# Root-mean-square factors of two norms computed on all partitions at once, through a product with ones and a power on GpSimd

## The chip, the cores and the metric

The kernel runs on one core of one Trainium2 chip. The metric is the device time of one execution in microseconds. A core has five engines that run side by side and meet only through semaphores: TensorE (PE) multiplies matrices into PSUM, VectorE (DVE) and ScalarE (ACT) read PSUM and SBUF, GpSimd (POOL) reads SBUF alone, and SyncE (SP) issues most of the transfers. Each takes its instructions in the order in which they are written for it.

## The reference

A two-layer block with sequence length 512 and width 1024: an attention with compressed, selected and windowed keys (NSA) and a latent attention (MLA) side by side, then an MLP. In float32 throughout. The parts that matter here are the norms:

```python
def rms_norm(x, g):
    xf = x.astype(jnp.float32)
    y = xf * lax.rsqrt(jnp.mean(xf * xf, axis=-1, keepdims=True) + EPS)
    return (y * g.astype(jnp.float32)).astype(x.dtype)

# in mla_attention: cq has 256 columns, ckv 128
q = (rms_norm(cq, q_norm) @ w_uq)...
kv = (rms_norm(ckv, kv_norm) @ w_ukv)...

# in reference, per layer
xn = rms_norm(x, attn_norm[l])
...
x = x + merged @ w_out[l]
hn = rms_norm(x, mlp_norm[l])
x = x + jnp.square(jax.nn.relu(hn @ w_up[l])) @ w_down[l]
# at the end
return rms_norm(x, final_norm)
```

## The kernel before

Everything lies transposed: a tile has 128 features on the partitions and the 512 positions along the columns, and x is eight such tiles. Each float32 operand of a product is split into a rounded half (fp32r, "hi") and a rest ("lo"), and `three` makes three products of them (hi·hi, hi·lo, lo·hi). A weight unit is 128x1024 float32, so one output tile of 512 columns is 8 x 3 = 24 products (`tile`, lines 1496 to 1498). SyncE loads units into a double buffer `stage` (the small ones of W1 and W2 into `stage_n`), ScalarE rounds them into `wsplit` (or `narrow`) and VectorE, in places GpSimd, subtracts for the rest (line 992, line 509). The next unit's load waits for that rest.

Per layer the stages are: the prefix (PREFIX in the code: projections KC, VC, KS, V, KW, Q0, CQ0, Q1, CQ1, W1, CQ2, ... up to the first gates, with the units W1,0 to W1,7 of the compression between them), 106 attention steps, the output projections, and the MLP as four quarters of eight "up" tiles and eight "down" tiles. The order on each engine is written out by hand as loops over the same lists.

A norm's factor differs per position, which here is per column, so it must stand on all partitions. Before, it comes about in five steps on four engines:

- the squares are summed over tiles into one 128x512 tile (`row_sum` for x; `csq` for the latents, where GpSimd adds the two tiles of cq, line 569);
- TensorE sums over the partitions: four fp32 products with one column of ones per tile turn the positions onto partitions (`mean_square`, line 1516; `c_mean_squares`, line 1637, eight products);
- ScalarE takes the root of that small block (`root`, line 642; `c_root`, line 738) and VectorE the reciprocal (lines 1026, 1123);
- VectorE writes it onto the diagonals of four 128x128 blocks (`norm_diagonals`, line 1029; `c_diagonals`, line 1127);
- TensorE spreads it over all partitions by an fp32 product of 512 columns with a matrix of ones (`spread`, line 1521; `c_spread`, line 1645, twice), and for x ScalarE copies it into `rs` (line 646). The latents are scaled straight from PSUM in `c_norm` (line 1135).

In the MLP the first quarter's tile 0 is followed by `mean_square`, and `spread` stands before the sixth of tile 1's eight steps. The tiles go into four banks in turn; on VectorE the first evacuation (line 1454: relu times `rs`) waits for `rs`. In its order there stand: the diagonals, the weight rest of tile 2, the wait for `rs`, evacuation 0, the rest of H 0 (line 1460, after ScalarE's square, line 964, and GpSimd's, line 611), evacuation 1, the weight rest of tile 3, and so on.

In the prefix, `c_square` follows each CQ tile, `c_mean_squares` the tile Q2 and `c_spread` the tile MISC. VectorE's order after MISC: evacuate (line 1051), key products, weight rest, query rests (line 996), key sum, the three `c_norm`, then the narrow rest for W1,4; at Q3 the rotation's first half (line 1067), the next weight rest, gates, hidden sum, rotation. GpSimd does the two key rests and the sum of line 569 and then waits to store gates to memory (line 515). The factor of the attention's norm and that of the last norm use the same functions `mean_square`, `root` and, for the first, `spread`.

## Time and profile before

| | |
|---|---|
| median of 3 runs | 1515.47 us (1514.43 to 1516.17) |
| the profiled execution | 1514.82 us, of which span 1513.0 us |
| granted TensorE clock, mean | 0.999 |
| busy: TensorE, VectorE, ScalarE, GpSimd | 1494.5, 891.1, 716.3, 437.5 us |
| instructions in the span | 21119 |

The span runs from the first to the last instruction that the profiler recorded; the rest of the execution's time lies around it. Busy times are sums of the durations of an engine's instructions. TensorE's are modelled and overlap, since products are pipelined: for what a product takes out of the stream the distance from start to start is read, not its duration. GpSimd's durations are rough.

### The profile page before, as it was taken

What the parts mean: (1) busy time and instruction counts of PE and PEld (TensorE: products, weight loads), DVE (VectorE), ACT (ScalarE), POOL (GpSimd) and SP (SyncE); (2) the same over time, 40 slices, a digit from 0 to 9 for tenths busy, and PEclk for the clock granted to TensorE, in tenths of its full rate; (3) what the DMA queues carried; (4) which work ended last, traced back from release to release, by engine and by line L of the source; (5) the groups of instructions that cost most, each with busy time, mean ns of one, the idle gap of its engine ahead of it and who ended that gap; (6) DMA issues with size and microseconds to landing.
All of it is one profiled execution on the core that took longest, in us unless ns stands there. A gap on an engine that the chain in (4) does not pass through costs nothing.

```text
span 1513.0 us, 21119 instructions
## 1 busy us (share of the span) xinstructions
PE 1494.5 (99%) x7332; PEld 1250.9 (83%) x7332; DVE 891.1 (59%) x1539; ACT 716.3 (47%) x1308; POOL 437.5 (29%) x459
## 2 busy tenths in 40 slices
PE   8999999999999999999999999999999999999998
PEld 6888888887888888888888888888888888888886
DVE  6876766767553544535557776667575535354453
ACT  6864777873431222222367557888544222122222
POOL 1302667773020101101022046778711101010111
PEclk9999999999999999999999999999999999999999
DMA  5344221135222333332323521212432233232333
GB/s 212 98 144 142 70 84 64 57 98 181 86 96 98 97 97 97 97 97 97 98 84 125 174 84 64 78 50 78 133 125 84 98 97 97 97 97 97 97 97 112
DMA packets 43362, 154.29 MB, mean 102 GB/s; under 512 B 5440, under 2 KB 5440, under 8 KB 43280
## 3 DMA queue, kind: packets, MB, share of 16 engines
q1 hardware_dynamic: 37296, 133.77, 27.6%
q0 software_dynamic: 5696, 18.94, 3.6%
q8 instruction: 47, 0.77, 0.2%
q10 hardware_dynamic: 288, 0.52, 0.1%
q14 instruction: 35, 0.29, 0.1%
HBM read 142.73 MB, written 10.49 MB: 101 GB/s over the span
## 4 chain that ended last, share of the span: by engine, by line
PE 87%; DVE 4%; ACT 4%; issue 3%; DMA 1%; POOL 1%; POOLq 0%; DVEq 0%; SPq 0%; ACTq 0%
PE G L1496 14%; PE G L1498 13%; PE G L1497 13%; PE O L1498 9%; PE O L1497 9%; PE O L1496 9%; PE O L1785 3%; PE T L1761 3%; PE S L1736 2%; PE T L1496 2%; PE T L1498 2%; PE T L1497 2%; ACT F L677 1%; PE O L1571 1%; PE S L1742 1%
## 5 line engine op out<-in xcount | busy, mean ns | idle before, releaser
L625 ACT ACTIVATE wsplit<-stage 128x1024 fp32r<-128x1024 f32 x227 | 240.3, 1058 | 598.8 <-PE G L1498 272.7
L992 DVE TENSOR_TENSOR wsplit<-stage,wsplit 128x1024 fp32r<-128x1024 f32 x180 | 262.7, 1460 | 72.9 <-ACT wsplit L625 72.6
L611 POOL TENSOR_TENSOR F<-Y 128x512 f32<-128x512 f32 x64 | 68.4, 1069 | 637.3 <-DVE Y L1454 637.3
L1496 PE MATMUL G<-xg,wsplit 128*128 128x512 f32 x560 | 223.7, 399 | 7.3 <-DVE wsplit L1018 6.9
L1497 PE MATMUL G<-xg,wsplit 128*128 128x512 f32 x560 | 219.3, 392 | 0.0
L1498 PE MATMUL G<-xg,wsplit 128*128 128x512 f32 x560 | 219.2, 391 | 0.0
L1229 DVE CUSTOM_DVE_ANT_0 F<-S,F 128x512 f32<-128x512 f32 x192 | 93.6, 488 | 94.8 <-PE S L1736 68.0
L509 POOL TENSOR_TENSOR wsplit<-stage,wsplit 128x1024 fp32r<-128x1024 f32 x46 | 111.4, 2421 | 125.6 <-ACT wsplit L625 125.1
L796 ACT ACTIVATE F<-F,nmx 128x512 f32<-128x512 f32 x192 | 107.7, 561 | 68.1 <-DVE nmx L1229 66.4
L1496 PEld LDWEIGHTS G<-xg,wsplit 128*128 128x128 f32 x560 | 105.7, 189 | 29.2 <-DVE wsplit L1018 6.9
L1496 PE MATMUL G<-area,wsplit 128*128 128x512 f32 x320 | 124.7, 390 | 0.2
L1498 PEld LDWEIGHTS G<-xg,wsplit 128*128 128x128 f32 x560 | 105.5, 188 | 23.0
L1496 PE MATMUL O<-area,wsplit 128*128 128x512 f32 x320 | 124.5, 389 | 0.0
L1498 PE MATMUL G<-area,wsplit 128*128 128x512 f32 x320 | 124.5, 389 | 0.0
L1498 PE MATMUL O<-area,wsplit 128*128 128x512 f32 x320 | 124.5, 389 | 0.0
L1497 PE MATMUL G<-area,wsplit 128*128 128x512 f32 x320 | 124.5, 389 | 0.0
L1497 PE MATMUL O<-area,wsplit 128*128 128x512 f32 x320 | 124.5, 389 | 0.0
L1497 PEld LDWEIGHTS G<-xg,wsplit 128*128 128x128 f32 x560 | 105.8, 189 | 20.5 <-issue 0.7
L1239 DVE TENSOR_TENSOR area_b<-T,area_b 128x512 fp32r<-128x512 f32 x192 | 92.7, 483 | 21.5 <-ACT area_b L791 20.2
L1496 PE MATMUL O<-xg,wsplit 128*128 128x512 f32 x256 | 99.6, 389 | 0.0
L1497 PE MATMUL O<-xg,wsplit 128*128 128x512 f32 x256 | 99.6, 389 | 0.0
L1498 PE MATMUL O<-xg,wsplit 128*128 128x512 f32 x256 | 99.6, 389 | 0.0
(292 smaller groups left out, 3044.3 us busy)
## 6 DMA issues: line engine op xcount, KB each, us to landing
stage<-units SPq DMA_DIRECT2D x229, 512.0 KB, 3.5
stage_n<-units_n SPq DMA_DIRECT2D x20, 512.0 KB, 3.9
gates<-Y POOLq DMA_DIRECT2D x32, 256.0 KB, 3.1
E<-gates POOLq DMA_DIRECT2D x24, 256.0 KB, 3.0
F<-gates POOLq DMA_DIRECT2D x8, 256.0 KB, 4.0
x<-x_in SPq DMA_DIRECT2D x3, 512.0 KB, 6.9
rope<-tables POOLq DMA_DIRECT2D x1, 768.0 KB, 6.4
out<-F SPq DMA_DIRECT2D x3, 256.0 KB, 2.3
```

Of the source, the lines that this page charges most:

```text
L509: pool.tensor_tensor(wslot(u)[:, 1, :], staged(u), wslot(u)[:, 0, :], ALU.subtract)\
L611: pool.tensor_tensor(F[:, m % 2, :], Y[:, m % 2, :], Y[:, m % 2, :], ALU.mult)\
L625: act.activation(wslot(u)[:, 0, :], staged(u), ACT.Copy).then_inc(s_whin if u in SN else s_whi, 1)
L796: act.activation(prob(i, w), prob(i, w), ACT.Exp, bias=nmx[:, i % 4:i % 4 + 1], scale=-1.0, accum_out=sums[:, i % 4:i % 4 + 1]).then_inc(s ...
L992: dve.tensor_tensor(wslot(u)[:, 1, :], staged(u), wslot(u)[:, 0, :], ALU.subtract)\
L1229: dve.tensor_tensor_reduce(prob(i, w), score_tile(i), maskrow[:, S - w:S], -1.0, 1e38, ALU.add, ALU.min, nmx[:, i % 4:i % 4 + 1]).then_inc ...
L1239: dve.tensor_tensor(pt_view(slot, 1, qt), tp_view(j % 2, qt), pt_view(slot, 0, qt), ALU.subtract)\
L1496: pe.matmul(dst, a(0), b(0), start=first, stop=False)
L1497: pe.matmul(dst, a(0), b(1), start=False, stop=False)
L1498: return pe.matmul(dst, a(1), b(0), start=False, stop=last)
L1761: ins = pe.transpose(TP[j % 2][:, kt * P:(kt + 1) * P], prob(j, S)[:, kt * P:(kt + 1) * P], ident)
L1785: ins = pe.matmul(dst[:, kt * P:S], v, PT[:, slot, c, kt * S:(kt + 1) * S - kt * P], start=opens and c == 0, stop=closes(j) is not None an ...
```

## The change

It leaves the attention's first norm and the last norm as they are, and makes the factors of the MLP norm and of the two latent norms in another way. The summed squares (128x512, still one sum per partition) are split into a rounded half on ScalarE and a rest on VectorE (MLP) or GpSimd (latents). Two fp32r products with a full matrix of ones, one for each half, accumulate into a PSUM bank in which every partition then holds the whole sum. VectorE writes sum / D + EPS from PSUM to SBUF, and GpSimd raises that tile of 512 columns to the power -1/2 with a `tensor_tensor` whose second operand is a constant -0.5, broadcast.

`mean_square`, `root`, the reciprocal, the diagonals and `spread` fall away for the MLP; `c_mean_squares`, `c_root`, `c_diagonals` and the fp32 products of `c_spread` for the latents. The two latent powers stand in GpSimd's order before its first gate store; `c_norm` reads the factor from SBUF and moves on VectorE from MISC to behind the evacuation and weight rest of the tile GATE 1, ahead of the narrow rest that follows there. The two fp32r products of the MLP stand where `spread` stood. The core of the diff:

```diff
-        ones = sb("ones", [P, P], F32)
+        ones_r = sb("ones", [P, P], R32)
-        crc = sb("crc", [P, 2, 2, QT], F32)
+        ones = ones_r[:, :].bitcast(F32)
+        CSQ = pcT[:, :, :, :].rearrange("p g c n -> p (g c) n")
+        SQ = area[:, 8192:9216].rearrange("p (c n) -> p c n", c=2)
+        minus_half = small[:, 1, 16:17]
...
@@ gpsimd
                 pool.tensor_tensor(csq[:, 0, :], csq[:, 0, :], csq[:, 1, :], ALU.add).then_inc(s_csum, 1)
+                pool.wait_ge(s_csqhi, l + 1)
+                pool.tensor_tensor(CSQ[:, 0:4:2, :], csq[:, 0:3:2, :], CSQ[:, 1:4:2, :], ALU.subtract).then_inc(s_csqlo, 1)
+                for kind in range(2):
+                    pool.wait_ge(s_cmean, l * 2 + (kind + 1))
+                    pool.tensor_tensor(csq[:, 2 * kind, :], csq[:, 2 * kind, :], minus_half.broadcast_to([P, S]), ALU.pow)\
+                        .then_inc(s_cfactor, 1)
                 for i in range(FIRST_GATE):
                     store_gate(i)
...
+                pool.wait_ge(s_wide, l + 1)
+                pool.tensor_tensor(rs[:, :], rs[:, :], minus_half.broadcast_to([P, S]), ALU.pow).then_inc(s_rsmlp, 1)
                 with pool.Fori(0, QUARTERS) as f:
@@ scalar
+            def squares_hi(l):
+                act.wait_ge(s_sqadd, l * (2 * KT) + 2 * KT)
+                act.activation(SQ[:, 0, :], F[:, 2, :], ACT.Copy).then_inc(s_sqhi, 1)
-                def c_root():
...
+                def c_squares_hi():
+                    act.wait_ge(s_csq, l * 3 + 3)
+                    act.wait_ge(s_csum, l + 1)
+                    act.activation(CSQ[:, 1:4:2, :], csq[:, 0:3:2, :], ACT.Copy).then_inc(s_csqhi, 1)
...
                     if item == ("Q", 2):
-                        c_root()
+                        c_squares_hi()
...
                         if isinstance(f, int) and m == 0:
-                            root(l * 2 + 1)
+                            squares_hi(l)
                         split_hi(l, U_MLP + m + 2, f)
-                        if isinstance(f, int) and m == 0:
-                            spread(l * 2 + 1)
@@ vector
+            def squares_lo(l):
+                dve.wait_ge(s_sqhi, l + 1)
+                dve.tensor_tensor(SQ[:, 1, :], F[:, 2, :], SQ[:, 0, :], ALU.subtract).then_inc(s_sqlo, 1)
+
+            def wide_mean(l):
+                dve.wait_ge(s_sqall, l + 1)
+                dve.tensor_scalar(rs[:, :], SB[0][:, :], 1.0 / D, EPS, ALU.mult, ALU.add).then_inc(s_wide, 1)
-                def c_diagonals():
...
+                def c_means():
                     for kind in range(2):
+                        dve.wait_ge(s_cspread, l * 2 + (kind + 1))
+                        ins = dve.tensor_scalar(csq[:, 2 * kind, :], g_tile(("CB", kind))[:, :], 1.0 / (128 if kind else 256),
+                                                EPS, ALU.mult, ALU.add)
+                        ins.then_inc(s_cmean, 1)
+                        dve.wait_ge(s_cmean, l * 2 + (kind + 1))
+                        dve.sem_inc(s_gfree, 1)
                 def c_norm(c):
-                    dve.wait_ge(s_cspread, l * 2 + (c // 2 + 1))
+                    dve.wait_ge(s_cfactor, l * 2 + (c // 2 + 1))
                     gain = par[:, PR_QN + c:PR_QN + c + 1]
-                    dve.scalar_tensor_tensor(E[:, c, :], E[:, c, :], gain, g_tile(("CB", c // 2))[:, :],
+                    dve.scalar_tensor_tensor(E[:, c, :], E[:, c, :], gain, csq[:, c // 2 * 2, :],
                                              ALU.mult, ALU.mult).then_inc(s_cf, 1)
...
                         key_sum()
-                        for c in range(3):
-                            c_norm(c)
+                        c_means()
...
+                    if item == ("GATE", 1):
+                        for c in range(3):
+                            c_norm(c)
...
                         if isinstance(f, int) and m == 0:
-                            norm_diagonals(l * 2 + 1)
+                            squares_lo(l)
                             split_lo(l, U_MLP + m + 2, f)
-                            dve.wait_ge(s_rs, l * 2 + 2)
+                            wide_mean(l)
+                            dve.wait_ge(s_rsmlp, l + 1)
@@ tensor
-                def c_mean_squares():
...
                 def c_spread(kind):
                     free(("CB", kind))
-                    pe.wait_ge(s_cdiag, l + 1)
-                    pe.matmul(g_tile(("CB", kind))[:, :], ones[:, :], csq[:, kind, :], start=True, stop=True)\
-                        .then_inc(s_cspread, 1)
+                    pe.wait_ge(s_csqlo, l + 1)
+                    for c in range(2):
+                        ins = pe.matmul(g_tile(("CB", kind))[:, :], ones_r[:, :], CSQ[:, 2 * kind + 1 - c, :], start=c == 0, stop=c == 1)
+                    ins.then_inc(s_cspread, 1)
...
-                    if item == ("Q", 2):
-                        c_mean_squares()
...
+                def wide_sum():
+                    pe.wait_ge(s_sqlo, l + 1)
+                    for c in range(2):
+                        ins = pe.matmul(SB[0][:, :], ones_r[:, :], SQ[:, c, :], start=c == 0, stop=c == 1)
+                    ins.then_inc(s_sqall, 1)
...
                         if isinstance(f, int) and m == 1:
-                            before = lambda k: spread(l * 2 + 1) if k == 5 else None
+                            before = lambda k: wide_sum() if k == 5 else None
                         tile(last_tile(m)[:, :], u, xg, before)
-                        if isinstance(f, int) and m == 0:
-                            mean_square(l * 2 + 1)
```

## Rows read from the trace of the kernel before

**Rows 1.** The page's engines: busy us, share of the span, instructions.
```profile
PE 1494.5 (99%) x7332; PEld 1250.9 (83%) x7332; DVE 891.1 (59%) x1539; ACT 716.3 (47%) x1308; POOL 437.5 (29%) x459
```

**Rows 2.** What TensorE waited for, whole span: us, times, longest us.
```profile
PE G L1496 <- DVE wsplit L1018: 6.9, 1, 6.9
...
PE O L1571 <- DVE narrow L992: 0.9, 2, 0.5
```

**Rows 3.** Timeline, TensorE, layer 0's MLP norm: start us, us, engine, line, instruction.
```profile
410.59 0.39 PE L1498 MATMUL G<-xg,wsplit 128*128 128x512 f32 x1
...
411.95 0.40 PE L1497 MATMUL G<-xg,wsplit 128*128 128x512 f32 x1
...
414.95 0.39 PE L1498 MATMUL G<-xg,wsplit 128*128 128x512 f32 x1
...
416.27 0.40 PE L1497 MATMUL G<-xg,wsplit 128*128 128x512 f32 x1
```

**Rows 4.** Timeline, TensorE, layer 0's latent sums and two W1 units.
```profile
81.47 1.84 PE L1637 MATMUL G<-ones,csq 128*128 128x1 f32 x16
83.17 1.21 PE L1571 MATMUL O<-narrow,area_b 128*128 128x256 f32 x8
...
98.55 1.19 PE L1571 MATMUL O<-narrow,area_b 128*128 128x256 f32 x8
```

**Rows 5.** GpSimd's groups by line and shape: busy us, mean ns | idle before.
```profile
L509 POOL TENSOR_TENSOR wsplit<-stage,wsplit 128x1024 fp32r<-128x1024 f32 x46 | 111.4, 2421 | 125.6 <-ACT wsplit L625 125.1
L611 POOL TENSOR_TENSOR F<-Y 128x512 f32<-128x512 f32 x64 | 68.4, 1069 | 637.3 <-DVE Y L1454 637.3
...
L569 POOL TENSOR_TENSOR csq<-csq 128x512 f32<-128x512 f32 x2 | 3.0, 1495 | 20.8 <-ACT csq L733 20.8
```

**Rows 6.** Timeline, MLP start of layer 0: VectorE's chain, TensorE's tile 3.
```profile
416.86 0.69 DVE L1454 SCALAR_TENSOR_TENSOR Y<-G,rs 128x512 f32<-128x512 f32 x1 [2.59 <-ACT rs L646]
...
419.99 1.22 DVE L992 TENSOR_TENSOR wsplit<-stage,wsplit 128x1024 fp32r<-128x1024 f32 x1
...
423.56 0.39 PE L1496 MATMUL O<-xg,wsplit 128*128 128x512 f32 x1
```

**Rows 7.** Timeline, prefix of layer 0: VectorE from MISC on, TensorE's seventh W1 unit.
```profile
89.89 0.69 DVE L1051 TENSOR_TENSOR E<-T,rs 128x512 f32<-128x512 f32 x1 [1.04 <-PE T L1498]
...
94.73 2.29 DVE L1135 SCALAR_TENSOR_TENSOR E<-E,par,G 128x512 f32<-128x512 f32 x3
97.17 1.23 DVE L992 TENSOR_TENSOR narrow<-stage_n,narrow 128x1024 fp32r<-128x1024 f32 x1 [0.15 <-DVE E L1135]
...
99.72 1.23 DVE L992 TENSOR_TENSOR wsplit<-stage,wsplit 128x1024 fp32r<-128x1024 f32 x1 [0.46 <-ACT wsplit L625]
...
115.01 1.23 DVE L992 TENSOR_TENSOR narrow<-stage_n,narrow 128x1024 fp32r<-128x1024 f32 x1 [0.52 <-ACT narrow L625]
...
118.09 1.11 PE L1571 MATMUL O<-narrow,area_b 128*128 128x256 f32 x8
```

**Rows 8.** One VectorE line (ns min/median/max), and timeline rows of a long one.
```profile
L1143 DVE TENSOR_TENSOR cn<-E,cn x6: 677/681/2119, 164.1 to 915.2; 128x512 fp32r<-128x512 f32 x6
...
165.36 2.40 POOL L509 TENSOR_TENSOR wsplit<-stage,wsplit 128x1024 fp32r<-128x1024 f32 x1 [2.17 <-ACT wsplit L625]
...
166.20 2.11 DVE L1143 TENSOR_TENSOR cn<-E,cn 128x512 fp32r<-128x512 f32 x1
```

**Rows 9.** ScalarE: table loads of the root's line; timeline of the last root.
```profile
L642 ACT ACT_TABLE_LOAD  x2: 1283/1283/1283, 407.9 to 1153.2; - x2
...
1501.72 0.63 ACT L630 ACTIVATE F<-x 128x512 f32<-128x512 f32 x1 [4.81 <-DVE x L1464]
1503.49 0.26 ACT L642 ACTIVATE rc<-S,small 128x4 f32<-128x4 f32 x1 [1.14 <-PE S L1915]
```

**Rows 10.** Timeline, TensorE, after the wait at the start.
```profile
8.34 0.63 PE L1496 MATMUL G<-xg,wsplit 128*128 128x512 f32 x1
8.77 0.63 PE L1497 MATMUL G<-xg,wsplit 128*128 128x512 f32 x1
```

More of the change, by code:

```diff
@@ L483, in _ @@
             pool.memset(vblk[:, :, :, :].bitcast(F32), 0.0).then_inc(s_init, 1)
+            pool.memset(minus_half, -0.5).then_inc(s_half, 1)
+            pool.wait_ge(s_half, 1)
             pool.wait_ge(s_x[3], 16)
@@ L844, in _ @@
                     act.wait_ge(s_par, l + 1)
-                    root(l * 2)
+                    root(l)
                     split_hi(l, BIG[3])
@@ L848, in _ @@
                     act.wait_ge(s_par, l + 1)
-                    root(l * 2)
+                    root(l)
                     split_hi(l, BIG[2])
@@ L853, in _ @@
                     if name == "VC":
-                        spread(l * 2)
+                        spread(l)
                         swap(0)
@@ L979, in _ @@
                     split_hi(l, NU + 1)
-            root(L * 2)
-            act.wait_ge(s_rec, L * 2 + 1)
+            root(L)
+            act.wait_ge(s_rec, L + 1)
             for b in range(0, KT, 2):
@@ L1628, in weights_T @@
                     ins.then_inc(s_cT, 1)
-                def c_mean_squares():
-                    free(("CM", 0))
-                    pe.wait_ge(s_csq, l * 3 + 3)
-                    pe.wait_ge(s_csum, l + 1)
-                    for kind, tiles in enumerate(((0,), (2,))):
-                        for tt in range(QT):
-                            for c in tiles:
-                                ins = pe.matmul(g_tile(("CM", 0))[:, QT * kind + tt:QT * kind + tt + 1],
-                                                csq[:, c, tt * P:(tt + 1) * P], ones[:, 0:1], start=c == tiles[0],
-                                                stop=c == tiles[-1])
-                    ins.then_inc(s_cms, 1)
                 def c_spread(kind):
                     free(("CB", kind))
-                    pe.wait_ge(s_cdiag, l + 1)
-                    pe.matmul(g_tile(("CB", kind))[:, :], ones[:, :], csq[:, kind, :], start=True, stop=True)\
-                        .then_inc(s_cspread, 1)
+                    pe.wait_ge(s_csqlo, l + 1)
+                    for c in range(2):
+                        ins = pe.matmul(g_tile(("CB", kind))[:, :], ones_r[:, :], CSQ[:, 2 * kind + 1 - c, :], start=c == 0, stop=c == 1)
+                    ins.then_inc(s_cspread, 1)
                 def gate(i, piece):
@@ L1692, in first_norm @@
                         pe.wait_ge(s_const, 48)
-                        mean_square(l * 2)
+                        mean_square(l)
                     if k == 4:
-                        spread(l * 2)
+                        spread(l)
                 for item in PREFIX:
@@ L1714, in _ @@
                     elif name == "VC":
-                        project(item, lambda k: spread(l * 2) if l > 0 and k == 2 else None)
+                        project(item, lambda k: spread(l) if l > 0 and k == 2 else None)
                     elif name == "KS":
```

43 lines of the change are left out of this document (15 added, 28 removed).

## The prediction

> **What bounds the kernel now.** I read the page's engine table first: TensorE is busy 99% of the span, VectorE 59%, ScalarE 47%, GpSimd 29% [rows 1]. Busy shares alone prove little, so next came the table of what TensorE waited for: one wait of 6.9 us at the very start, and after it only small ones, 0.9 us in all for the largest line [rows 2]. So TensorE's stream sets the time nearly everywhere, and an edit is worth what it takes out of that stream, as long as no other engine becomes late by it. The small waits of [rows 2] on `narrow` are a warning: in the prefix (the projections ahead of the attention) VectorE delivers the weight rests of the W1 units only just in time. Then I read the timelines of the two places that the change touches, TensorE first and then the engines that feed it. All times below are on the clock of the profiled execution; layer 1 repeats layer 0 some 745 us later.
>
> **Removed and added on TensorE, MLP norm.** Products of the normal kind follow each other every 0.227 us (0.2265 measured over a tile; 24 make a tile of 5.44 us). From the last product of tile 0 to the second of tile 1 there are 1.36 us [rows 3], where two steps would be 0.45: the four fp32 column sums cost 0.91 us. Around the fp32 spread it is 1.32 us [rows 3], so the spread costs 0.87. In their place come two fp32r products of 512 columns, 2 x 0.227 = 0.45. TensorE gains 0.91 + 0.87 - 0.45 = 1.32 us per layer (the pass over `ones` as 128 weights is no new form).
>
> **The same for the latents.** The eight fp32 column sums start at 81.47 and the next unit at 83.17 [rows 4]: 1.70 us. The two spreads, at 0.87 each, are 1.73; four fp32r products replace them, 0.91. That is 1.70 + 1.73 - 0.91 = 2.52 us per layer. If all of it arrived: 2 x (1.32 + 2.52) = 7.7 us, 0.5%. The rest of the sum is what this uncovers.
>
> **The price of the power, X.** No row shows a power on GpSimd. Its cheapest two-input pass over 128x512 is 1.07 us, a less favourable one 1.50 [rows 5]. The low end is 1.07: the power also reads two operands per column, so a price under that of a multiplication is excluded. It can't be one ALU step, though: a logarithm, a multiplication and an exponential are at least three. I take three passes of the 1.50 row, X = 4.5 us, and for the high end six of them, 9.0 us, as the polynomials and special cases may need more. Nothing in the trace narrows this further, and the answer hangs on it, so I carry X through. (The Trainium skill, GPSIMD Engine Reference, section "Performance versus the Vector engine", says that data-dependent branching costs about 12 cycles per element there; at the 1.2 GHz of that page that would be an estimate of 5.1 us for 512 columns, and the sum below would come out at 1530. No run here shows it; it speaks against this change.)
>
> **MLP norm with X.** The squares' rounding goes to ScalarE (0.63 us) and the rest to VectorE (0.69 us) as soon as the sum is there, near 408.6; both are done by 410, and the products that need them come at 414.3, so they cost nothing. (If ScalarE were late there, the products would wait with all of TensorE behind them; the margin is 4 us.) The table load that stood in that place is gone. The two products end near 414.9, VectorE's mean takes 0.69 like the evacuation of [rows 6] and ends at 415.6, GpSimd starts 0.08 later, and the row factors are there at 415.75 + X. Before, they were used at 416.86 [rows 6]. Behind that wait VectorE has queued: the first evacuation, a rest of H, the second evacuation, and the weight rest for tile 3. From the first start to the last end it is 419.99 + 1.22 - 416.86 = 4.35 us [rows 6]. Tile 3 began at 423.56 [rows 6] and would now begin at 423.56 - 1.32 = 422.24. So the cover holds up to X = 422.2 - 4.35 - 415.75 = 2.1 us; each us more is a us of TensorE, once per layer (later tiles have 5.44 us each and VectorE needs 2.7). Per layer: -1.32 + (X - 2.1).
>
> **Latents with X.** First the small losses. GpSimd's subtraction of two rows is a 128x1024 operation, 2.4 us [rows 5], from some 84.05 to 86.45; TensorE asks for it at 88.0, so it is covered, but a rotation on VectorE just before its end meets it (about 0.2 us). VectorE was free for MISC at 88.85, 1.04 us ahead of TensorE's 89.89 [rows 7]; now it is free at 89.1 and TensorE was done before, so MISC is only 0.8 us sooner while TensorE is 1.7 sooner. The gate transposes wait for its key product (0.4 us), the W1 unit before them 0.2. So TensorE reaches the end of Q3 1.9 us sooner (96.45), not 2.5; with the small wait before 98.55 [rows 4] also gone, 2.1 sooner at best.
>
> Second, **the shared port**. A 128x512 subtraction on VectorE with both inputs in SBUF has a median of 681 ns and a maximum of 2119 [rows 8]; the long one began at 166.20, while a GpSimd subtraction ran from 165.36 for 2.40 us, and ended at 168.31, half a microsecond after it [rows 8]. It was simply held until GpSimd's instruction ended. If a power holds the port in the same way, VectorE's weight rests are held for X, twice. The mean for kind 0 ends at 94.6 (94.73 [rows 7] less 0.8, plus 0.69); the first power runs from 94.7 to 94.7 + X; the narrow rest for the next W1 unit (at 97.17 before, [rows 7]) is held and ends at 95.8 + X, where TensorE wanted it at 96.45. Then the second power gets the port and holds the next weight rest, which ends at 96.9 + 2X (before: 99.72 + 1.23 = 100.95, [rows 7]). Behind it stand the hidden sums, ScalarE's tanh and swap, the rotation of Q3 and from there a nearly unbroken run of VectorE work up to the narrow rest at 115.01 [rows 7]; all of that moves by 2X - 4.1. In that run the three latent scalings now stand too (2.29 us, [rows 7], with 0.5 us idle to eat), so that rest ends at 118.0 + (2X - 4.1), and TensorE wanted it at 118.09 [rows 7]. TensorE's shift at that point is the larger of X - 2.7 and 2X - 4.2, per layer. The stores of the gates in GpSimd's queue behind the two powers begin only at 110.7, those cost nothing up to X of about 7. What VectorE saves (reciprocal and diagonals, 1.6 us at 84) lies in its idle time.
>
> **The tail.** Square roots remain at the start of each layer and at the end, tanh and exp lie between, so table loads (1.28 us each, [rows 9]) are as many as before but two of them move: one to the start of layer 1, where ScalarE idles 2 us, and one ahead of the last root. There ScalarE is free at 1502.35 and the root began at 1503.49 [rows 9]; with the load it begins at 1503.63: +0.15 us.
>
> **The sum** with X = 4.5: latents 2 x (9.0 - 4.2) = +9.6; MLP 2 x (-1.32 + 2.4) = +2.2; tail +0.15; together +11.9. In general 6X - 15.1 for X over 2.1. The profiled execution took 1514.82 us (span 1513.0), so 1526.7. The median of the runs is 0.65 us above that, 0.04%, less than I can foresee. At X = 9.0 it is +38.9, 1553.7. At X = 1.07: latents 2 x (X - 2.7), MLP 2 x -1.32, tail 0.15, -5.8, 1509.0. One thing is left out of the sum: after its 6.9 us of idleness at the start TensorE issued ten products 0.43 us apart, the pace of 1.2 GHz, before it reached 0.23 (the granted clock shows full speed there) [rows 10]. Ten such products cost 2.0 us; two to four long waits could add 4 us or more, which I put on the high end only.
>
> **Rivals.** *The power is cheap* (this is the faster side). If X is below 1.97, the time falls by over 3 us: at 1.5 it is 4 x 1.5 - 10.9 = -4.9, 1509.9. For it: an ordinary pass is 1.07 to 1.50 [rows 5] and a hardware path for the power would cost no more; against it: three elementary functions in one pass. Break-even is X = 2.5. *The power takes its time but does not hold the port.* If it computes long per column and reads little, VectorE's rests could slip through. Then the latents keep their 2.1 us per layer and only the MLP pays: 2X - 10.9, which at 4.5 is -1.9, 1512.9, no measurable change; faster below 3.9, slower above 6.9. The held subtraction of [rows 8] speaks against it, but its blocker was a streaming operation. (The Trainium skill, Advanced Engine Details and Errata, section "Mode Summary", says that the second VectorE port is shared and that the two engines block each other; the trace agrees for ordinary operations, 2.11 us against 0.68.) *The power is far dearer* than six passes: above 1554, each further us of X costs 6.
>
> **Chances.** Forecast, X between 3 and 9 with the port held: 0.46. Dearer still: 0.14. Port held and X between 2 and 3, within the band: 0.05. Cheap power: 0.22. Port not held and X over 2: 0.13, of which 0.04 faster, 0.07 within, 0.02 slower. That makes 0.26 faster by more than 0.2% (3 us, about what a measurement of this kernel can tell from none), 0.12 within, 0.62 slower. The range runs from the cheap power, 1509, to the high end with the slow restarts, 1558; it leaves out most of "dearer still" and a little at the bottom.
>
> **What will show it.** The new GpSimd group's mean duration is X, the first thing to look up. Right: VectorE subtractions near 96 and 98 us that last X instead of 1.2 us and end with the power; TensorE waiting on `narrow` ahead of the fifth and the seventh W1 unit; in the MLP a TensorE wait on `wsplit` of X - 2.1 ahead of tile 3, twice. Wrong: rests of normal length during a power (the port), no wait ahead of tile 3 (the price), an fp32r product of the sums that takes more than 0.23 us of the stream, or a third place that waits. The forecast falls most easily by X alone.

## The result, and the profile after

The changed kernel takes 1963.91 us (median of 5 runs, 1963.21 to 1965.11); the kernel before, on the same chip, takes 1515.03. The ratio is 1.296, 95% interval 1.295 to 1.298. The direction was the one forecast, the size was not: I had said 1526.7, with 1558 as the upper end.

The page of the changed kernel: the engines (busy us, share, instructions), and in 40 slices of the span how busy TensorE was, in tenths, and the clock it was granted.

```profile
PE 1494.7 (76%) x7284; PEld 1250.9 (64%) x7284; DVE 891.5 (45%) x1537; ACT 716.8 (37%) x1304; POOL 936.0 (48%) x468
...
PE   8930079999950899999999100999999309999998
...
PEclk9975589999985899999999655999999759999999
```

Against [rows 1], TensorE, VectorE and ScalarE have the same work as before, to a tenth of a per cent. Only GpSimd has more, 936.0 us for 437.5. TensorE's share falls to 76% because its stream now stands still in four stretches, two per layer. The same in the table of TensorE's waits (us in all, times, longest):

```profile
PE O L1594 <- DVE narrow L1009: 289.2, 6, 143.9
PE O L1519 <- DVE wsplit L1009: 159.4, 2, 79.7
```

And in GpSimd's groups (busy us, mean ns | idle before):

```profile
L582 POOL TENSOR_TENSOR csq<-csq,small 128x512 f32<-128x512 f32 x4 | 327.7, 81932 | 16.1 <-DVE csq L1149 16.1
L621 POOL TENSOR_TENSOR rs<-rs,small 128x512 f32<-128x512 f32 x2 | 163.9, 81944 | 109.1 <-DVE rs L1047 109.1
```

One power over 512 columns takes 81.94 us. A multiplication over the same columns (line 611, a square) was 1.07 us in [rows 5]. The waits are the two that the prediction named, at some 30 times the size forecast; in [rows 2] the one on `narrow` was 0.9 us in all, and the other did not appear.

The prefix of layer 0, timeline (start us, us; in brackets the idle time before and what ended it), VectorE, GpSimd and TensorE:

```profile
93.82 163.85 POOL L582 TENSOR_TENSOR csq<-csq,small 128x512 f32<-128x512 f32 x2 [8.04 <-DVE csq L1149]
94.73 1.23 DVE L1009 TENSOR_TENSOR narrow<-stage_n,narrow 128x1024 fp32r<-128x1024 f32 x1 [0.15 <-DVE csq L1149]
96.10 1.18 PE L1594 MATMUL O<-narrow,area_b 128*128 128x256 f32 x8 [0.30 <-DVE narrow L1009]
...
175.81 2.20 DVE L1158 SCALAR_TENSOR_TENSOR E<-E,par,csq 128x512 f32<-128x512 f32 x2 [64.04 <-POOL csq L582]
257.71 0.75 DVE L1158 SCALAR_TENSOR_TENSOR E<-E,par,csq 128x512 f32<-128x512 f32 x1 [79.70 <-POOL csq L582]
258.38 1.22 DVE L1009 TENSOR_TENSOR narrow<-stage_n,narrow 128x1024 fp32r<-128x1024 f32 x1
259.65 2.08 PE L1594 MATMUL O<-narrow,area_b 128*128 128x256 f32 x8 [143.86 <-DVE narrow L1009]
```

The two powers fill GpSimd from 93.82 to 257.67. The narrow rest at 94.73 runs inside the first of them and takes its usual 1.23 us, so the power does not hold VectorE back. TensorE's W1 unit follows at 96.10, where [rows 4] has it at 98.55. Not all of these 2.5 us come from the new sums: the last product ahead of them starts at 80.73, where before it was 81.25, so 0.5 us of the lead was there already, and the stage has gained 1.9 us. The stop comes later. VectorE is ready for `c_norm(0)` at 111.77, idles 64.04 us for the first power and 79.70 us for the second. Right behind `c_norm(2)` in its queue stands the narrow rest (258.38) that TensorE has wanted since 115.79.

Layer 0's MLP norm:

```profile
559.34 81.94 POOL L621 TENSOR_TENSOR rs<-rs,small 128x512 f32<-128x512 f32 x1 [54.55 <-DVE rs L1047]
641.32 0.69 DVE L1477 SCALAR_TENSOR_TENSOR Y<-G,rs 128x512 f32<-128x512 f32 x1 [82.06 <-POOL rs L621]
644.44 1.22 DVE L1009 TENSOR_TENSOR wsplit<-stage,wsplit 128x1024 fp32r<-128x1024 f32 x1
645.71 0.79 PE L1519 MATMUL O<-xg,wsplit 128*128 128x512 f32 x1 [79.70 <-DVE wsplit L1009]
646.30 0.63 PE L1520 MATMUL O<-xg,wsplit 128*128 128x512 f32 x1
...
649.63 0.40 PE L1519 MATMUL O<-xg,wsplit 128*128 128x512 f32 x1
```

Here the chain is the one of [rows 6]: from 641.32 to 644.44 + 1.22 it is again 4.34 us, and tile 3 begins just after. The wait is 79.70, that is X - 2.24. The products then start 0.43 us apart, as in [rows 10]: nine intervals from 645.71 to 649.63 last 3.92 us where nine of 0.227 are 2.04, so the stop costs another 1.9 us. A window of the same trace (start:end, length, busy us of PE, PEld, DVE, ACT and POOL, granted clock, DMA share, GB/s) shows a mean granted clock of 0.61 of full speed, so mostly the 1.2 GHz level, after 79.70 us of waiting:

```profile
641.00:652.00 11.00, 6.29 (x20) 5.04 (x21) 6.23 (x8) 3.78 (x5) 5.12 (x4) 0.61 0.30 89
```

### The profile page after: what moved, and what is told of

Its sections match the earlier page's. It is cut to its first block, busy times and chain, and to the rows that moved or that the text cites. A ratio compares the mean times of both kernels' runs of the same rounds, so it can differ in the third digit from the quotient of the medians.

```text
span 1961.4 us, 21025 instructions
## 1 busy us (share of the span) xinstructions
PE 1494.7 (76%) x7284; PEld 1250.9 (64%) x7284; DVE 891.5 (45%) x1537; ACT 716.8 (37%) x1304; POOL 936.0 (48%) x468
## 4 chain that ended last, share of the span: by engine, by line
PE 59%; issue 23%; POOL 9%; DVE 4%; ACT 4%; DMA 1%; POOLq 0%; DVEq 0%; SPq 0%; ACTq 0%
PE G L1519 9%; PE G L1521 9%; PE G L1520 9%; POOL csq L582 8%; PE O L1519 6%; PE O L1520 6%; PE O L1521 6%; PE O L1795 3%; PE T L1771 3%; PE S L1746 2%; PE T L1519 1%; PE T L1520 1%; PE T L1521 1%; ACT F L698 1%; PE O L1594 1%
## 5 line engine op out<-in xcount | busy, mean ns | idle before, releaser
L582 POOL TENSOR_TENSOR csq<-csq,small 128x512 f32<-128x512 f32 x4 | 327.7, 81932 | 16.1 <-DVE csq L1149 16.1
L1594 PE MATMUL O<-narrow,area_b 128*128 128x256 f32 x128 | 20.3, 306 | 289.2 <-DVE narrow L1009 289.2
L1519 PE MATMUL O<-xg,wsplit 128*128 128x512 f32 x256 | 101.4, 396 | 159.4 <-DVE wsplit L1009 159.4
L621 POOL TENSOR_TENSOR rs<-rs,small 128x512 f32<-128x512 f32 x2 | 163.9, 81944 | 109.1 <-DVE rs L1047 109.1
L1594 PEld LDWEIGHTS O<-narrow,area_b 128*128 128x128 f32 x128 | 18.4, 207 | 293.0 <-DVE narrow L1009 290.9
L1519 PEld LDWEIGHTS O<-xg,wsplit 128*128 128x128 f32 x256 | 48.9, 191 | 170.4 <-DVE wsplit L1009 160.2
L1158 DVE SCALAR_TENSOR_TENSOR E<-E,par,csq 128x512 f32<-128x512 f32 x6 | 5.9, 1007 | 287.5 <-POOL csq L582 287.5
L830 ACT ACTIVATE Y<-Y 128x512 f32<-128x512 f32 x32 | 19.9, 622 | 298.9 <-DVE Y L1076 296.4
L1520 PE MATMUL O<-area,wsplit 128*128 128x512 f32 x320 | 124.5, 389 | 0.0
L1519 PE MATMUL O<-area,wsplit 128*128 128x512 f32 x320 | 124.5, 389 | 0.0
```

Source lines behind the costliest of these rows:

```text
L582: pool.tensor_tensor(csq[:, 2 * kind, :], csq[:, 2 * kind, :], minus_half.broadcast_to([P, S]), ALU.pow)\
L621: pool.tensor_tensor(rs[:, :], rs[:, :], minus_half.broadcast_to([P, S]), ALU.pow).then_inc(s_rsmlp, 1)
L1519: pe.matmul(dst, a(0), b(0), start=first, stop=False)
L1520: pe.matmul(dst, a(0), b(1), start=False, stop=False)
```

## The experiments

My theory after the result: the whole loss is the duration of the power, in two places, and the rest of the change is a gain. The rivals: the fp32r sums or their roundings cost something too; the place of `c_norm` in VectorE's order, or GpSimd's queue, makes the long wait; the power is slow only for these values, this exponent or this operand form.

### The whole change, the power replaced by a multiplication (e1_mult)

```diff
-            pool.memset(minus_half, -0.5).then_inc(s_half, 1)
+            pool.memset(minus_half, 0.002).then_inc(s_half, 1)
...
-  pool.tensor_tensor(rs[:, :], rs[:, :], minus_half.broadcast_to([P, S]), ALU.pow)
+  pool.tensor_tensor(rs[:, :], rs[:, :], minus_half.broadcast_to([P, S]), ALU.mult)
```

(and the same for the two powers over `csq`; the factors are then no roots).

> The three powers per layer are replaced by multiplications of the same tiles with a small constant (0.002 in place of -0.5), so the factors of the MLP and latent norms are not the reference's. Theory A (the power's price of 81.9 us is the whole loss, and the fp32r sums give what the prediction's sum said): each GpSimd pass is 1.1 to 1.5 us, no long wait is left, and the time is 1507 to 1510, that is 5.5 to 8 us below the kernel before. Rival B (the new order of waits, the moved scalings or the fp32r products cost by themselves): 1515 or more. Rival C (an ordinary multiplication holds the port, as a subtraction did before, and the narrow rest is late): in between, near 1511, with narrow rests of about 2 us beside the GpSimd pass.

Measured: 1508.67 us (1508.40 to 1509.03), before 1515.56, ratio 0.9955 (0.9942 to 0.9969). GpSimd's group of the latents' factors:

```profile
L582 POOL TENSOR_TENSOR csq<-csq,small 128x512 f32<-128x512 f32 x4 | 6.1, 1537 | 16.1 <-DVE csq L1149 16.1
```

TensorE's wait in the prefix:

```profile
PE O L1594 <- DVE narrow L1009: 1.5, 4, 0.4
```

At this price the change is 6.9 us faster than before by the medians, 6.1 by the profiled executions (1514.82 to 1508.70). The prediction's low end, worked out for X = 1.07, was 5.8 below the profiled execution. Set product against product, TensorE's stream gains 1.9 us per layer in the latents and 1.4 in the MLP norm, where the prediction's low end had 1.6 and 1.3. So no other term of the change costs more than the sum allowed for it. (The latents' multiplications took 1.54 us each and not 1.07; TensorE doesn't wait for them.)

### Each half alone (e2_mlp_only, e3_latents_only)

The first keeps the new MLP norm and restores the latents' path of before, the second the reverse:

```diff
e2, against the changed kernel:
-                        c_means()
+                        for c in range(3):
+                            c_norm(c)
...
+                    if item == ("Q", 2):
+                        c_mean_squares()
...
e3, against the changed kernel:
-                            before = lambda k: wide_sum() if k == 5 else None
+                            before = lambda k: spread(l * 2 + 1) if k == 5 else None
...
+                        if isinstance(f, int) and m == 0:
+                            mean_square(l * 2 + 1)
```

> Only the MLP norm is changed, the latent norms are those of before. Theory A: TensorE waits 81.9 - 2.2 = 79.7 us per layer ahead of tile 3 and restarts slowly (2 us), less the 1.3 us gained: 2 x 80.2 = +160, 1675 us. Rival D (the two places are not independent, a delay of one hides part of the other): more than 165 over the kernel before.

> Only the latent norms are changed. Theory A: two powers in a row, 163.9 us, less some 20 us that VectorE's order has between the start of the first and its scalings: a wait of 144 us per layer, plus 2 us of slow restart, less 2.5 gained: 2 x 143.4 = +287, 1802 us. Rival D: the sum of this and the MLP alone differs from the whole change's +449 by more than 5 us.

Measured: 1676.16 us (ratio 1.106, 1.104 to 1.108) and 1803.81 us (1.190, 1.189 to 1.192). TensorE's longest wait of each, the MLP alone first and then the latents alone:

```profile
PE O L1519 <- DVE wsplit L1006: 159.4, 2, 79.7
```

```profile
PE O L1579 <- DVE narrow L1003: 289.3, 6, 143.8
```

The losses against before (1515.56, same chip) are 160.6 and 288.3, together 448.9, and the whole change loses 1963.91 - 1515.03 = 448.9. The two places don't touch each other.

### What sets the price of the power (e6_price)

A kernel of its own: powers over a growing number of columns, then with other partitions, values, exponents and operand forms, and beside them VectorE's passes.

```diff
+            pool.tensor_tensor(w[0][:, 64:128], sq[:, 64:128], half(64), ALU.pow)
+            pool.tensor_tensor(w[0][:, 128:256], sq[:, 128:256], half(128), ALU.pow)
...
+            pool.tensor_tensor(w[1][0:16, 0:128], sq[0:16, 0:128], half(128, 16), ALU.pow)
+            pool.tensor_tensor(w[2][:, 0:128], one[:, 0:128], half(128), ALU.pow)
...
```

> No part of the reference is computed: GpSimd powers, multiplications and VectorE operations on one 128x512 tile, the output is zeros. Theory A: a power costs 0.16 us per column and nothing else that matters: 4 columns 0.7, 8 columns 1.3, 64 columns 10.2, 128 columns 20.5, 256 columns 41 us. Open: whether it depends on the number of partitions (16 instead of 128: same if each column is a step of all lanes, an eighth if lanes are served in turn), on the values (all ones), on the exponent (2, 1) or on a broadcast second operand (a full tile of -0.5). Port: while a 128-column power runs, VectorE's two-input subtractions over 128x512 last 0.6 to 0.7 us each (the power does not hold the port) if the trace of the changed kernel is read rightly; while three GpSimd multiplications run they last over 1 us.

Timeline of that kernel, GpSimd's operations one after the other, then VectorE's beside a power (185.81), beside GpSimd's full-tile multiplication (205.18), and its reciprocals:

```profile
6.30 1.01 POOL L52 TENSOR_TENSOR w<-sq,mh 128x4 f32<-128x4 f32 x1
7.28 10.52 POOL L53 TENSOR_TENSOR w<-sq,mh 128x64 f32<-128x64 f32 x1
17.76 20.73 POOL L54 TENSOR_TENSOR w<-sq,mh 128x128 f32<-128x128 f32 x1
38.45 41.12 POOL L55 TENSOR_TENSOR w<-sq,mh 128x256 f32<-128x256 f32 x1
79.54 20.71 POOL L56 TENSOR_TENSOR w<-sq,mh 16x128 f32<-16x128 f32 x1
100.22 20.71 POOL L57 TENSOR_TENSOR w<-one,mh 128x128 f32<-128x128 f32 x1
...
183.02 1.03 POOL L61 TENSOR_TENSOR w<-sq,mh 128x512 f32<-128x512 f32 x1
...
185.81 0.69 DVE L94 TENSOR_TENSOR v<-sq,one 128x512 f32<-128x512 f32 x1
205.18 1.68 DVE L98 TENSOR_TENSOR v<-sq,one 128x512 f32<-128x512 f32 x1 [8.72 <-POOL w L65]
213.51 10.13 DVE L104 RECIPROCAL v<-sq 128x512 f32<-128x512 f32 x3
```

From 128 to 256 columns the power grows by 20.39 us, 0.159 us per column; 512 columns make 81.9, which is X. The multiplication of the same form takes 1.03 for 512. Sixteen partitions cost as much as 128, a tile of ones as much as the squares. The powers with exponent 2, with exponent 1 and with a full tile of exponents took 20.70, 20.71 and 20.76. So none of these cases is cheap, and only fewer columns help. Other ways to write the power (`tensor_scalar` with the exponent as a constant, another type, or VectorE in GpSimd's place) were not run.

### Fewer partitions (e13_lanes)

```diff
+            for i, rows in enumerate((16, 8, 4, 2, 1, 12, 17, 24, 32, 64, 128)):
+                pool.tensor_tensor(w[i if i < 10 else 11][0:rows, 0:64], sq[0:rows, 0:64], half(64, rows), ALU.pow)
```

> No part of the kernel: its outputs are zeros and nothing of the reference is computed; it measures the price of the power over 64 columns for 16, 8, 4, 2, 1, 12, 17, 24, 32, 64 and 128 partitions. Known from the price run: 10.5 us for 128 partitions and 64 columns, and 20.7 us for 128 columns with 128 as with 16 partitions. Theory: within a group of 16 partitions the elements are taken one after the other. Then 8 partitions take 5.4 us, 4 take 2.9, 1 takes 1.0, and 12 take 8.0, while 17, 24, 32, 64 and 128 take 10.5. Rival: sixteen partitions are computed side by side by a long series of steps. Then every one of the eleven takes 10.5 us. (The Trainium skill, GPSIMD Engine Reference, section Performance versus the Vector engine, gives about 12 cycles per element for data-dependent branching; if that is counted for each of 16 partitions in turn, an estimate at that page's 1.2 GHz is 0.16 us per column, which is the measured price.)

GpSimd's groups of it, one partition and 128:

```profile
L51 POOL TENSOR_TENSOR w<-sq,mh 1x64 f32<-1x64 f32 x1 | 10.5, 10513 | 0.0
...
L51 POOL TENSOR_TENSOR w<-sq,mh 128x64 f32<-128x64 f32 x1 | 10.5, 10513 | 0.0
```

All eleven took 10.51 to 10.52 us. My theory missed: unused partitions save nothing. The run fits the rival, a long series of steps for all partitions at once. It doesn't exclude a loop over sixteen lanes that never skips one; that stays open, and for a kernel it is the same price.

### Half of the columns (e5_half)

```diff
-  pool.tensor_tensor(rs[:, :], rs[:, :], minus_half.broadcast_to([P, S]), ALU.pow)
+  pool.tensor_tensor(rs[:, 0:256], rs[:, 0:256], minus_half.broadcast_to([P, 256]), ALU.pow)
+  pool.tensor_tensor(rs[:, 256:512], rs[:, 256:512], little.broadcast_to([P, 256]), ALU.mult)
```

> The power is taken over 256 of the 512 columns; the other 256 are multiplied by a small constant in a second GpSimd instruction, so half of the positions have other factors than the reference's. Theory A (the price is 0.16 us per column, no fixed part): a power of 41.0 us, waits per layer of 41.0 + 0.6 - 2.2 = 39.4 in the MLP and 2 x 41.6 - 20 = 63 in the prefix; with 4 us of slow restarts and 3.8 us gained, 2 x 102.6 = +205, 1720 us. Rival E (a fixed cost per power, such as loading code, is a large part of the 82 us): powers of clearly more than 41 us, and a time over 1740.

Measured: 1723.06 us (ratio 1.137), powers of 41.13 us, and TensorE's waits:

```profile
PE O L1598 <- DVE narrow L1013: 128.4, 6, 63.4
PE O L1523 <- DVE wsplit L1013: 79.0, 2, 39.5
```

With the multiplication of the other half, about 0.6 us, X is 41.7. The waits are then 2X - 20 and X - 2.2, the same offsets as in the changed kernel (143.86 and 79.70 at X = 81.94). In the changed kernel the offset of 20 is the 22.0 us from the first power's start (93.82) to the time from which TensorE wants the rest (115.79), less the 2.0 us from the second power's end to TensorE's restart. A large fixed cost per power is ruled out: 41.13 is half of 81.94 to 0.2 us.

### The prediction's own prices (e11_x4p5, e12_x9)

The powers over 20 and over 48 columns, the rest multiplied, otherwise as in the last diff. X is 3.55 + 1.00 = 4.55 and 8.03 + 0.95 = 8.98 us in the MLP.

> The whole change at the price that the prediction took: each power runs over 20 columns only and the other 492 are multiplied by 0.002 (so the factors of those columns are wrong: this part of the computation is left out), together about 4.5 us. It tests the rest of the sum at its own price. The prediction's sum, 6X - 15.1, says 1526.7. If the port is never held by the power and c_norm finds its factors ready (the wait of the changed kernel, 143.86, is 2 x 81.93 less 20, so it is nought up to 10 us), only the MLP pays X - 2.2 per layer: 1508.7 + 4.6 = 1513.3, and TensorE's waits in the prefix stay below 2 us.

> As the last, with the powers over 48 columns and the multiplication over 464, together about 9 us, the upper bound that the prediction took. (The factors of the 464 columns are wrong again.) The prediction's sum says 1553.7. By the waits of the changed kernel, 2X - 20 in the latents and X - 2.2 in the MLP: nought and 6.8 per layer, 1508.7 + 13.5 = 1522.2, and up to 2 us more where the latents' threshold is a little lower or where TensorE starts again slowly. A slope of 2 us per us of X between the two runs shows that only the MLP pays; a slope of 6 would be the prediction's.

Measured: 1516.04 us (11 runs, 1515.05 to 1517.07; before there 1514.57, ratio 1.0009, 1.0000 to 1.0018) and 1527.74 us (ratio 1.0084, 1.0070 to 1.0097). The prediction's sum gave 1526.7 and 1553.7. TensorE at 4.5, its largest wait but for the start's, and from the timeline two products of layer 1's restart:

```profile
PE O L1523 <- DVE wsplit L1013: 4.6, 2, 2.3
```

```profile
1167.87 0.50 PE L1523 MATMUL O<-xg,wsplit 128*128 128x512 f32 x1 [2.29 <-DVE wsplit L1013]
...
1169.02 0.63 PE L1524 MATMUL O<-xg,wsplit 128*128 128x512 f32 x1
```

The same at 9, where the timeline rows are the first slow product and the first one past the slow stretch:

```profile
PE O L1523 <- DVE wsplit L1013: 13.4, 2, 6.7
```

```profile
427.16 0.79 PE L1523 MATMUL O<-xg,wsplit 128*128 128x512 f32 x1 [6.72 <-DVE wsplit L1013]
...
430.98 0.40 PE L1523 MATMUL O<-xg,wsplit 128*128 128x512 f32 x1
```

In the prefix TensorE waits 1.5 and 2.0 us in all: nothing of the prediction's latents term is there. The MLP waits are as expected, 2.3 and 6.7 per layer. Yet both runs lie above what I expected, by 2.7 and 5.5 us. The slow restarts are most of it. At 9, nine intervals from 427.16 to 430.98 take 3.82 us instead of 2.04, and in layer 1 3.49 (1178.84 to 1182.33). At 4.5 the pace after the 2.3 us wait stays 0.23 in layer 0, and in layer 1 it drops to 0.43 for some eight products: twelve intervals from 1167.87 to 1172.32 take 4.45 instead of 2.72. The window over the slow products, in the same form as above:

```profile
1168.60:1172.30 3.70, 3.70 (x10) 2.87 (x10) 2.48 (x4) 0.63 (x1) 1.97 (x2) 0.54 0.48 142
```

The granted clock is 0.54 there, so nearly all of it at the 1.2 GHz level, and 1.00 in the windows ahead of it (1165 to 1168) and behind it (1172.3 to 1176). From the multiplication's span, 1506.9, the books close to half a microsecond: 1506.9 + 4.6 + 1.7 = 1513.2 against a span of 1513.8, and 1506.9 + 13.4 + 0.5 (what the prefix waits more) + 1.8 + 1.4 = 1524.0 against 1524.5. Per us of X the two runs differ by 2.6 us in the medians, and by 2.0 in the waits ahead of tile 3 alone; the prediction's slope was 6.

### `c_norm` later in VectorE's order (e10_norm_later)

```diff
-                    if item == ("GATE", 1):
-                        for c in range(3):
-                            c_norm(c)
...
+                    if name == "W2K":
+                        for c in range(3):
+                            c_norm(c)
```

> The whole change with GpSimd's powers, and only the three c_norm moved in VectorE's order: from after GATE 1's evacuation to the item W2K, behind the narrow rest that W1,6 waits for. The theory that c_norm's place makes the prefix's wait of 143.9 us, and that GpSimd's own queue holds nothing urgent: the wait shrinks by the work that lies between the two places, and the time falls to 1800 to 1900. Rival, GpSimd's queue: the gate stores stand behind both powers and the evacuations of the next gates wait for them, so that TensorE stops elsewhere for about as long: 1950 to 1964, the wait carried by another line.

Measured: 1961.81 us (1961.42 to 1963.94). Timeline, TensorE's restart and VectorE's first evacuation of a gate behind it:

```profile
258.74 0.61 PE L1636 MATMUL G<-area_b,area 128*128 128x64 f32 x2 [142.22 <-DVE area_b L1188]
...
259.81 0.69 DVE L1076 TENSOR_TENSOR Y<-G,rs 128x512 f32<-128x512 f32 x1 [1.47 <-DMA gates<-Y]
```

My theory missed. TensorE gets one unit further and then stands as long, for the next rest in VectorE's queue (`area_b`, behind `c_norm`). The rival's number is right and its mechanism only in part: the evacuation at 259.81 does wait for a gate store that stood behind both powers, but for 1.47 us more. In these two orders VectorE's queue decides which row carries the wait, and the end of the second power, 257.4, decides how long it is. What the gate stores alone would cost is not shown: no run has them ahead of the powers.

### The same sums with other ways to the factor (e7_root, e9_logexp)

First, ScalarE's square root over 512 columns straight from PSUM, and VectorE's reciprocal over 512:

```diff
+                act.activation(rs[:, :], SB[0][:, :], ACT.Sqrt, scale=1.0 / D, bias=eps).then_inc(s_wide, 1)
...
-                dve.tensor_scalar(rs[:, :], SB[0][:, :], 1.0 / D, EPS, ALU.mult, ALU.add).then_inc(s_wide, 1)
+                dve.reciprocal(rs[:, :], rs[:, :]).then_inc(s_rsmlp, 1)
```

> The fp32r sums stay; the power is replaced by a square root over 128x512 on ScalarE straight from PSUM (scale 1/D, bias EPS) and a reciprocal over 128x512 on VectorE; GpSimd has no part in it. Theory A: nothing of the 449 us is left, TensorE's gain of 3.8 us per layer arrives but for small waits: 1507 to 1510 us, faster than both kernels. The reciprocal's price over 512 columns is the unknown: no row shows one over more than 16 columns; if it is near 0.7 us like other passes, no cost; if it goes like the difference between 2 columns (0.16 us) and 16 (0.25), about 7 ns a column or 3.5 us, it moves the first MLP evacuation to some 419 on the clock of before, past the cover of 417.8: 1 us more per layer, and near 1511.

Measured: 1525.50 us (ratio 1.0073, 1.0059 to 1.0087). VectorE's group:

```profile
L1157 DVE RECIPROCAL csq<-csq 128x512 f32<-128x512 f32 x4 | 13.1, 3324 | 0.1
```

TensorE's wait in the prefix:

```profile
PE O L1598 <- DVE narrow L1016: 11.0, 4, 5.1
```

My theory missed, by 15 us. A reciprocal over 512 columns is 3.3 us of VectorE, 6.5 ns per column, near the price that I had taken from its short rows, and in the MLP it costs what I expected, 1.1 us of waiting per layer. What I had not worked out is the prefix: two of them stand ahead of the narrow rest there. Against the run with multiplications TensorE loses 6.7 us in layer 0's prefix and 7.1 in layer 1's, waits and slow pace behind them, and 1.4 per layer in the MLP. That turns the 6.9 us gain into an 11 us loss.

Then no division at all: exp(-ln(mean + EPS) / 2), both on ScalarE, `c_norm` at W2K, the two products with ones ahead of tile 1's second step.

```diff
+                act.activation(rs[:, :], SB[0][:, :], ACT.Ln, scale=1.0 / D, bias=eps).then_inc(s_wide, 1)
+                act.wait_ge(s_wide, l + 1)
+                act.activation(rs[:, :], rs[:, :], ACT.Exp, scale=-0.5).then_inc(s_rsmlp, 1)
...
-                            before = lambda k: wide_sum() if k == 5 else None
+                            before = lambda k: wide_sum() if k == 1 else None
```

> The whole change, but no power on GpSimd: the factor (mean + EPS)^(-1/2) is formed on ScalarE over 512 columns as exp(-ln(mean + EPS)/2), the logarithm straight from the PSUM bank of sums. The three c_norm run at the item W2K, behind the narrow rest that the next product waits for; in the MLP the two products with ones go before tile 1's second step. My theory (the power's duration is the whole loss, the fp32r sums themselves are a gain): the time of the run in which the powers were multiplications, 1508.7, give or take 3; faster than the kernel before by 0.3 to 0.7%, and no wait of TensorE's above 2 us in either place. Rival, ScalarE takes the bound: its table loads (1.28 us each) and four more passes of 512 columns per layer delay its roundings; then 1512 to 1520, with waits of PE for DVE narrow or ACT wsplit of 2 to 5 us.

Measured: 1507.59 us (1507.40 to 1508.70), before 1515.01, ratio 0.9954 (0.9941 to 0.9968). It is faster than both kernels, 7.4 us below the one before. Timeline of layer 0's MLP norm, ScalarE and VectorE's first use:

```profile
409.42 1.28 ACT L665 ACT_TABLE_LOAD   x1
410.71 0.69 ACT L665 ACTIVATE rs<-S,small 128x512 f32<-128x512 f32 x1
411.42 1.28 ACT L667 ACT_TABLE_LOAD   x1
412.71 0.63 ACT L667 ACTIVATE rs<-rs 128x512 f32<-128x512 f32 x1
413.38 0.69 DVE L1486 SCALAR_TENSOR_TENSOR Y<-G,rs 128x512 f32<-128x512 f32 x1 [2.72 <-ACT rs L667]
```

TensorE's wait in the prefix:

```profile
PE O L1603 <- DVE narrow L1026: 1.0, 2, 0.5
```

Factor and two table loads take 409.42 to 413.34, 3.9 us, all in ScalarE's idle time, and VectorE's first use at 413.38 is 3.5 us ahead of [rows 6]. Some 2.7 us of that lead come from the earlier place of the two products (four steps of three products at 0.227 us). The rival, ScalarE as the new bound, doesn't show. The run changes the factor, the place of `c_norm` and the place of the sums together, so what each is worth isn't separated.

## Why the prediction was wrong, and where it was right

**The step that failed is "the price of the power, X".** I took three passes of the 1.50 row (an addition), 4.5 us, and six for the upper end, 9.0. It measures 81.94, 55 passes of that row and 77 of the multiplication's 1.07. No row of before showed a power, and the bound from above wasn't one: "six passes" counted how many simple steps a power has and took each at a streaming row's pace, and nothing in the trace said that the steps stream. Since the price per us was known to be about 6, an unbounded X meant an unbounded upper end. I gave "far dearer" 0.14 and left it outside the range.

The page's figure that I set beside it did no better. (The Trainium skill, GPSIMD Engine Reference, section "Performance versus the Vector engine": about 12 cycles per element with data-dependent branching; counted per column it gave an estimate of 5.1 us. The measurement decides: 0.159 us per column, at that page's 1.2 GHz an estimate of 191 cycles, sixteen times the figure. Counted for each of the 16 partitions of a core it would come out right, but one partition costs as much as sixteen, so no run shows that this is why.)

**The shared port: wrong as a term, right as a rival.** I let the power hold VectorE's rests because a streaming subtraction does [rows 8]. Beside the power the subtraction takes 0.69 us and the rest 1.23, as always. At X near 4.5 the forecast says 1526.7 and the rival "does not hold the port" 1512.9; the run gives 1516.0. At X near 9 they say 1553.7 and 1521.9, and the run 1527.7. Most of what lies above the rival is the slow restarts (1.7 and 3.2 us), which I had put on the high end only.

**The latents' wait: right place, wrong mechanism.** The predicted threshold, 2X - 4.2, came from rests held by the port. The measured wait is 2X - 20, at X = 41.7 and at 81.94: VectorE waits for the factor at `c_norm`, and the narrow rest for the seventh W1 unit stands behind it. Ahead of the fifth unit, where I had forecast a wait too, TensorE idles 0.30 us. My rival without the port said that the latents never pay. It holds in the runs at 4.5 and 9; it is wrong at 41.7 and 81.94, and by 2X - 20 from about 10 on. I had no case in which `c_norm` itself is late. That 6X - 15.1 would have given 1991 us at X = 81.94, near the 1963.9 measured, is luck: the slope of 6 is right for another reason.

**The MLP: right.** A threshold of 2.1 against 2.24 measured, one us of TensorE per us of X, and the chain of 4.35 us again 4.34.

**TensorE's gains: right.** Predicted -5.8 at a multiplication's price, measured -6.1 by the profiled executions, 1.9 us per layer in the latents (I had 2.1 at best, and 1.6 with a port held for 1.07 us) and 1.4 in the MLP (I had 1.3).

**The budget of the change**, in spans: 1506.9 with multiplications, + 287.7 (the wait on `narrow`, 289.2 less 1.5), + 159.4 (the wait on `wsplit`), + the four restarts, is 1961.3; the span is 1961.4. Product against product beside the run with multiplications, the restarts cost 2.0 and 1.9 us in layer 0 (prefix, MLP) and 1.7 and 1.7 in layer 1.

## What to carry to other kernels

An operation that no row shows has no upper bound from rows of other operations: multiply its possible price by the slope, and if one case breaks the kernel, measure that operation alone before it stands on a path. Of the three ways tried here to a factor over 512 columns, the logarithm and exponential on ScalarE, which idles in that place, cost least (0.69 + 0.63 us and two table loads of 1.28); VectorE's reciprocal is 3.3 us, a root on ScalarE ahead of it, and GpSimd's power 82. When a new result is consumed in an in-order queue, ask what stands behind the consumer: here the bound engine waited for that, and not for the consumer.

## What the runs showed of the hardware that I had not expected

- GpSimd's power costs 0.16 us per column (20.39 us from 128 to 256 columns) in all cases tried: 1 to 128 partitions, squares or ones, three exponents. For 4 columns it is 1.01 us.
- A wait as short as 2.3 us can be followed by the slow pace. In the 4.5 us run one layer went on at full pace after it and the other lost about 1.7 us. After 6.7 us and after 79.7 us it was there in both layers, and cost between 1.4 and 1.9 us.
- Each streaming pass of GpSimd over 512 columns that was tried holds VectorE, not only one with two full tiles; the power doesn't. That was the question of a last run:

```diff
+            stage(0, lambda i: pool.tensor_tensor(t[i][:, 0:32], sq[:, 0:32], half(32), ALU.pow))
...
+            stage(2, lambda i: pool.tensor_tensor(w[3 + i][:, :], sq[:, :], half(512), ALU.mult))
+            stage(3, lambda i: pool.tensor_tensor(w[6 + i][:, :], sq[:, :], one[:, :], ALU.mult))
+            stage(4, lambda i: pool.tensor_scalar([w[9], w[11], f0][i][:, :], sq[:, :], 2.0, 1.0, ALU.mult, ALU.mult))
```

> No part of the kernel: its outputs are zeros and nothing of the reference is computed; it measures prices. Six stages; in each, GpSimd runs three operations (a power over 32 columns with a broadcast exponent; a power over 32 columns with a tile as exponent; a multiplication 128x512 by a broadcast operand; one by a full tile; a tensor_scalar 128x512; a multiplication of a tile with itself), and VectorE runs beside them subtractions of two 128x512 tiles and tensor_scalar over 512 columns. Theory: what holds VectorE's two-input pass is GpSimd reading two full tiles at the rate of a pass. So VectorE's subtraction takes 0.69 us beside both powers and beside the multiplication by a broadcast operand, and 1.5 to 1.8 us beside the full-tile multiplication and the square. Rival, any wide pass of GpSimd holds it: also 1.5 us or more beside the broadcast multiplication and the tensor_scalar.

Its timeline, VectorE beside the power, and beside GpSimd's multiplication by a broadcast operand:

```profile
6.00 0.69 DVE L91 TENSOR_TENSOR v<-sq,one 128x512 f32<-128x512 f32 x1
...
37.87 1.42 DVE L91 TENSOR_TENSOR v<-sq,one 128x512 f32<-128x512 f32 x1 [12.64 <-POOL w L65]
39.32 1.15 DVE L92 TENSOR_SCALAR v<-sq 128x512 f32<-128x512 f32 x1
```

Beside the broadcast multiplication VectorE's subtraction takes 1.42 us instead of 0.69, and its one-input pass 1.15 instead of 0.43. Beside full tiles it was up to 1.63 and 1.37, beside GpSimd's tensor_scalar up to 0.97 and 0.72, and beside either form of the power 0.69 and 0.43. So the rival was right for the multiplication (1.42 where it said 1.5 or more), and the tensor_scalar lies between. (The Trainium skill, Advanced Engine Details and Errata, section "Mode Summary", says that VectorE's second port is shared and that GpSimd's instructions and VectorE's two-port ones block each other, which is narrower than I put it in the prediction. The multiplication's rows agree in that VectorE is held, the power's don't; which of VectorE's two passes is a two-port one no run here shows.)
